# Expert rows of a two-layer mixture kernel: scattered by slot through HBM instead of gathered by one-hot matmuls, with a new order of the dense ranks and of the weight splitting

## What is computed

```python
def moe(h, p):
    t = h.reshape(B * L, D)
    scores = jax.nn.sigmoid(jnp.dot(t, p['router_w'], preferred_element_type=F32))
    biased = (scores + p['router_b'].astype(F32)).reshape(-1, N_GROUPS, epg)
    grp = jnp.argmax(lax.top_k(biased, TOP_K)[0].sum(-1), -1)
    in_grp = jnp.take_along_axis(biased, grp[:, None, None], axis=1)[:, 0]
    _, local = lax.top_k(in_grp, TOP_K)
    expert = grp[:, None] * epg + local
    w = jnp.take_along_axis(scores, expert, -1)
    w = ROUTE_SCALE * w / w.sum(-1, keepdims=True)
    combine = (jax.nn.one_hot(expert, N_EXPERTS, dtype=F32) * w[..., None]).sum(1)
    hid = jax.nn.silu(jnp.einsum('td,edf->tef', t, p['moe_w_gate'])) * jnp.einsum('td,edf->tef', t, p['moe_w_up'])
    y = jnp.einsum('tef,efd->td', hid * combine[..., None].astype(hid.dtype), p['moe_w_down'])
```

## Time and profile before

| | value |
|---|---|
| median of three runs | 1816.57 us |
| the profiled execution's own time | 1820.26 us |
| its span | 1818.1 us |
| mean granted TensorE clock | 0.911 of full speed |
| TensorE (PE) busy | 1561.1 us, 86% |
| VectorE (DVE) busy | 903.4 us, 50% |
| ScalarE (ACT) busy | 720.1 us, 40% |
| GpSimd (POOL) busy | 189.1 us, 10% |
| moved by DMA | 271.78 MB, mean 149 GB/s |

### The profile page before, as it was taken

The page is one execution under the profiler, slowest core; times in us unless marked ns, Lnnn a source line. Parts: engine busy times, 40 slices in busy tenths (PEclk is TensorE's granted clock), DMA queues, the critical chain, the costliest instruction groups (busy, mean ns, idle before and its releaser), DMA issues.

```text
span 1818.1 us, 29285 instructions
## 1 busy us (share of the span) xinstructions
PE 1561.1 (86%) x9368; PEld 1291.0 (71%) x9368; DVE 903.4 (50%) x1591; ACT 720.1 (40%) x1215; POOL 189.1 (10%) x226
## 2 busy tenths in 40 slices
PE   6999988889996698888779999898899958898884
PEld 4888877676885576666568789777678747676672
DVE  1754634424346544565837445443343474545656
ACT  3453334341244434455244433434222453435543
POOL 0010100000000532101000110000000013430010
PEclk9999988899998699999859989888999978999896
DMA  9412143432351247876262222435233404668640
GB/s 343 141 62 90 47 172 114 168 110 98 116 182 35 110 157 244 317 265 233 88 254 105 70 70 95 148 117 180 75 128 122 165 1 151 215 231 328 246 152 35
DMA packets 74523, 271.78 MB, mean 149 GB/s; under 512 B 9452, under 2 KB 9756, under 8 KB 72832
## 3 DMA queue, kind: packets, MB, share of 16 engines
q1 hardware_dynamic: 66384, 236.79, 37.0%
q0 software_dynamic: 7984, 33.07, 4.8%
HBM read 254.97 MB, written 16.19 MB: 149 GB/s over the span
## 4 chain that ended last, share of the span: by engine, by line
PE 58%; DVE 17%; DMA 8%; ACT 6%; issue 4%; DVEq 4%; ACTq 1%; SPq 0%; POOL 0%; POOLq 0%
PE psum L982 6%; PE psum L983 6%; PE psum L984 6%; PE psum L1359 4%; DMA ring<-units_in 4%; PE psum L1539 3%; DVE ring_lo L2217 3%; PE psum L1480 3%; DMA ring<-units_ada 3%; PE psum L1481 3%; PE psum L1482 3%; DVE ring_lo L2308 2%; ACT w_hi L1765 2%; PE psum L1518 1%; PE psum L1001 1%
## 5 line engine op out<-in xcount | busy, mean ns | idle before, releaser
L2308 DVE TENSOR_TENSOR ring_lo<-ring,u_hi 128x1024 fp32r<-128x1024 f32 x116 | 143.8, 1239 | 329.2 <-ACTq L1849 325.0
L982 PE MATMUL psum<-x_hi,u_hi 128*128 128x384 f32 x736 | 264.1, 359 | 21.4 <-DVEq L2310 10.8
L984 PE MATMUL psum<-x_hi,ring_lo 128*128 128x384 f32 x736 | 254.5, 346 | 0.0
L983 PE MATMUL psum<-x_lo,u_hi 128*128 128x384 f32 x736 | 254.5, 346 | 0.0
L1848 ACT ACTIVATE u_hi<-ring 128x1024 fp32r<-128x1024 f32 x116 | 122.8, 1058 | 280.7 <-DMA ring<-units_in 202.5
L982 PEld LDWEIGHTS psum<-x_hi,u_hi 128*128 128x128 f32 x736 | 145.2, 197 | 36.9 <-issue 11.5
L983 PEld LDWEIGHTS psum<-x_lo,u_hi 128*128 128x128 f32 x736 | 145.2, 197 | 1.5 <-issue 0.3
L984 PEld LDWEIGHTS psum<-x_hi,ring_lo 128*128 128x128 f32 x736 | 144.4, 196 | 0.0
L2217 DVE TENSOR_TENSOR ring_lo<-ring,w_hi 128x1024 fp32r<-128x1024 f32 x96 | 118.2, 1231 | 40.9 <-ACTq L1766 32.8
L1765 ACT ACTIVATE w_hi<-ring 128x1024 fp32r<-128x1024 f32 x96 | 101.7, 1059 | 42.0 <-PE psum L1520 24.3
L1061 PE MATMUL psum<-ring,condS 128*32 128x128 f32 x1536 | 68.6, 320 | 39.3 <-DMA ring<-units_ada 37.8
(11 more groups left out here) (415 smaller groups left out, 3222.5 us busy)
## 6 DMA issues: line engine op xcount, KB each, us to landing
ring<-units_moe SPq DMA_DIRECT2D x132, 512.0 KB, 5.2
ring<-units_in SPq DMA_DIRECT2D x116, 512.0 KB, 3.4
ring<-units_ada SPq DMA_DIRECT2D x96, 512.0 KB, 4.9
R<-units_moe SPq DMA_DIRECT2D x60, 512.0 KB, 6.4
ring<-units_br SPq DMA_DIRECT2D x32, 320.0 KB, 2.9
ring<-units_out SPq DMA_DIRECT2D x16, 512.0 KB, 3.3
expert_out_rows<-RE POOLq DMA_DIRECT2D x12, 512.0 KB, 6.5
prm<-params SPq DMA_DIRECT2D x2, 1304.0 KB, 10.0
```

The costliest lines, as they stand in the source:

```text
L982: mm(o, hi[:, c], x_hi[:, k, :], start=k == 0, stop=False)
L983: mm(o, hi[:, c], x_lo[:, k, :], start=False, stop=False)
L984: i = mm(o, lo[:, c], x_hi[:, k, :], start=False, stop=k == DT - 1)
L2308: V.tensor_tensor(ring_lo[:, slot_of(u), :], ring[:, slot_of(u), :, :].rearrange("p a b -> p (a b)"), u_hi[:, n % 2, :].bitcast(F32), ALU. ...
```

## The change

The one-hot gather, its constants and matrices, and the stage `hl` are gone. In their place:

- The stage `hb` turns the unsplit rows (24 transposes) into `h2_rows`. VectorE writes the integer slots, and POOL scatters all rows by slot into an HBM tensor, `slot_rows`, with six indirect DMAs. It waits for all of them and then loads the rows of 15 tiles (12 of FULL ranks, 3 for all SMALL ranks) one after the other, three ahead, into `rows_in`. In the first layer the tensor is filled once with finite values, in 15 DMAs during the mixers, at the stage `rs`.
- Steps `("xt", x)` turn a tile by eight transposes on TensorE; ScalarE writes the high part and VectorE the low part (SMALL: one copy each for a half of the k-tiles).
- VectorE, not POOL, forms the low part of the dense rows (`low_of_h2`), in pieces between the routing steps.
- Rank 0 goes first, ahead of rank 2. Its down product times its weight becomes the accumulator `acc` (`take_first`). Rank 1 stays last.
- The step `back` stands behind the last rank's second gate-up half and ahead of its `tr`. VectorE alone adds the rows that came back, and the gated sum, for all three tiles.
- `rounded_at` skips steps whose units are all SMALL. So where the next rank is SMALL, the down units of a FULL rank are split at the rank's own `("gu", r, 1)`.
- Banks for the jobs are chosen by their count of jobs.

```diff
-ORDER = [2, 11, 3, 12, 4, 13, 10, 14, 5, 15, 9, 6, 8, 7, 0, 1]
+ORDER = [0, 2, 11, 3, 12, 4, 13, 10, 14, 5, 15, 9, 6, 8, 7, 1]
+FIRST, LAST = ORDER[0], ORDER[-1]
...
+def turned_in(before, r):
+    if r == FIRST:
+        return FULL_TILES[0:2]
+    if before == FIRST:
+        return SMALL_ROWS
+    q = ORDER[ORDER.index(r) + 1]
+    return [(q, t) for t in range(len(TILES[q]))] if q in FULL else []
...
 def expert_steps():
-    first, second = ORDER[:2]
-    s = [("ga", 1, 0, 4), ("ga", 1, 4, DT), ("gu", first, 0), ("gu", first, 1), ("ga", 0, 0, DT)]
-    for before, r in zip(ORDER[:-2], ORDER[1:-2]):
-        s += [("gu", r, 0), ("tr", before)] + ([("ga",) + FILL[r]] if r in FILL else [])
-        s += [("gu", r, 1), ("dn", before)]
-    before, r = ORDER[-3:-1]
-    s += [("gu", r, 0), ("tr", before), ("g2",), ("dn", before), ("gu", r, 1)]
-    s += [("gu", LAST, 0), ("back",), ("tr", r), ("dn", r), ("gu", LAST, 1)]
+    def turned(before, r):
+        return [("xt", x) for x in turned_in(before, r)]
+    s = [("gu", FIRST, 0)] + turned(None, FIRST) + [("gu", FIRST, 1)]
+    for before, r in zip(ORDER[:-2], ORDER[1:-1]):
+        s += [("gu", r, 0), ("tr", before)] + turned(before, r) + [("gu", r, 1), ("dn", before)]
+    before = ORDER[-2]
+    s += [("gu", LAST, 0), ("tr", before), ("dn", before), ("g2",), ("gu", LAST, 1), ("back",)]
     return s + [("tr", LAST), ("dn", LAST)]
...
 def rounded_at():
-    at = {i: [] for i in range(len(STEPS))}
-    with_units = [1] + [i for i, step in enumerate(STEPS) if step_units(step)]
+    at = {i: [] for i in range(-1, len(STEPS))}
+    with_units = [-1] + [i for i, step in enumerate(STEPS) if any(u in ROUND_AT for u in step_units(step))]
     for i, j in zip(with_units, with_units[1:]):
         at[i] = [u for u in step_units(STEPS[j]) if u in ROUND_AT]
...
+            def turn_tile(x):
+                i = ROW_AT[x]
+                pe.wait_ge(rows_loaded[i % IN_PLACES], nth(l, rows_loaded[i % IN_PLACES], 16 * (i // IN_PLACES + 1)))
+                for half, job in enumerate(step_jobs(("xt", x))):
+                    turn_rows(job, [rows_in[:, i % IN_PLACES, (4 * half + k) * P:(4 * half + k + 1) * P] for k in range(4)])
...
+                        if l == 0:
+                            for at in range(0, N_SLOT, P):
+                                n = min(P, N_SLOT - at)
+                                pool.dma_start(slot_rows[at:at + n, :], cst[0:n, 0:D]).then_inc(rows_cleared, 16)
...
-                for d in range(DT):
-                    pool.wait_ge(x_hi_ready, nth(l, x_hi_ready, DT + d + 1))
-                    nc.gpsimd.tensor_tensor(h_lo[:, d, :], h2[:, d, :], h_hi[:, d, :].bitcast(F32), ALU.subtract)
+                pool.wait_ge(back_ready, nth(l, back_ready, 2 * NT))
                 pool.wait_ge(slots_ready, nth(l, slots_ready, 1))
...
+                for t in range(NT):
+                    for x in range(2):
+                        n = x * NT + t
+                        pool.indirect_dma_start(
+                            out=slot_rows, out_offset=bass.IndirectOffsetOnAxis(ap=slot_i[:, n:n + 1], axis=0),
+                            in_=h2_rows[:, t, :], in_offset=None,
+                            bounds_check=N_SLOT - 1, oob_is_err=False).then_inc(scattered, 16)
+                pool.wait_ge(scattered, nth(l, scattered, 16 * 2 * NT))
+                for i in range(IN_PLACES):
+                    load_rows(i)
...
             def add_back(t):
-                dve.wait_ge(scaled_ready, nth(l, scaled_ready, t + 1))
                 dve.wait_ge(rows_back[t], nth(l, rows_back[t], 32))
+                dve.wait_ge(acc_ready, nth(l, acc_ready, t + 1))
+                for x in range(2):
+                    V.scalar_tensor_tensor(out=acc[:, t, :], in0=back_rows[x][:, t, :], scalar=wab[:, x, t:t + 1],
+                                           in1=acc[:, t, :], op0=ALU.mult, op1=ALU.add)
+                    dve.drain()
...
+            def gated_sum(t):
+                V.tensor_tensor(acc[:, t, :], acc[:, t, :], g2bc[:, min(t, 1), :], ALU.mult)
                 dve.drain()
-                V.scalar_tensor_tensor(out=X[:, t, :], in0=X[:, t, :], scalar=ALPHA, in1=acc,
+                V.scalar_tensor_tensor(out=X[:, t, :], in0=X[:, t, :], scalar=ALPHA, in1=acc[:, t, :],
                                        op0=ALU.mult, op1=ALU.add)
...
+            def take_turned(x):
...
+                for half, job in enumerate(jobs):
+                    dve.wait_ge(xg_hi_ready, nth(l, xg_hi_ready, 2 * i + half + 1))
+                    k = slice(4 * half, 4 * half + 4)
+                    V.tensor_tensor(lo[:, k, :].rearrange("p a b -> p (a b)"), psum[:, bank(job), :],
+                                    hi[:, k, :].rearrange("p a b -> p (a b)").bitcast(F32),
+                                    ALU.subtract).then_inc(drained[bank(job)], 1)
...
                 elif name == "rt":
+                    for d in range(3):
+                        low_of_h2(d)
...
+                    for d in range(3, 5):
+                        low_of_h2(d)
...
                     for x, v in enumerate((low, top)):
-                        V.tensor_tensor(hot_at[:, x, :, :], along(v).to_broadcast(pair),
-                                        across(route_const("chunk_base")).to_broadcast(pair), ALU.subtract)
+                        V.tensor_copy(slot_i[:, x * NT:(x + 1) * NT], v)
                     dve.drain().then_inc(slots_ready, 1)
...
+                    for d in range(5, DT):
+                        low_of_h2(d)
```

More of the change, by code:

```diff
@@ L181, in stages @@
           ("rl", [], ["rl"]),
[L182 to L184 removed]
+          ("hb", [], [f"hb{t}{h}" for t in range(NT) for h in range(2)]),
+          ("cn", [], ["cn"])]
     return s
@@ L263, in token_tiles @@
         return [(t * P, 0, P, None) for t in range(NT)]
-    c, off, width = CHUNK_OF[r], SLOT_OFF[r], HALF if r in SMALL else P
-    out, done = [], 0
-    while done < SPAN[r]:
-        at = min(off + done, CHUNK_W[c] - width)
-        if done:
-            at = min(at, max(off, off + SPAN[r] - width))
-        row = off + done - at
-        n = min(SPAN[r] - done, width - row)
-        out.append((at, row, n, CHUNK_BASE[c] + off + done))
-        done += n
-    return out
+    if r in SMALL:
+        at = min(SLOT_OFF[r], N_SMALL - HALF)
+        return [(at, SLOT_OFF[r] - at, CAP[r], SLOT_OFF[r])]
+    return [(0, 0, min(P, CAP[r] - at), SLOT_OFF[r] + at) for at in range(0, CAP[r], P)]
 TILES = {r: token_tiles(r) for r in range(N_EXPERTS)}
@@ L322 @@
 ROUNDED_AT = rounded_at()
-def gather_parts(c):
-    return ("x",) if CHUNKS[c] == SMALL else ("h", "l")
 def step_jobs(step):
@@ L333, in step_jobs @@
         return [f"tr{step[1]}.{t}" for t in range(len(TILES[step[1]]))]
-    if step[0] == "ga":
-        return [f"ga{step[1]}.{k}{x}" for k in range(step[2], step[3]) for x in gather_parts(step[1])]
+    if step[0] == "xt":
+        return [f"xt{ROW_AT[step[1]]}.{half}" for half in range(2)]
     if step[0] == "back":
@@ L483, in route_constants @@
     e = np.arange(N_EXPERTS)
[L484 to L486 removed]
+    base = [ABSENT * 2 if r in DENSE else SLOT_OFF[r] for r in range(N_EXPERTS)]
+    c = {"before": i < j, "ones": np.ones(P), "expert": e, "key_tie": N_EXPERTS - 1 - e,
+         "rank": e, "slot_base": np.array(base)}
     return np.ascontiguousarray(np.concatenate(
@@ L1455, in gate_up @@
                 jobs = step_jobs(("gu", r, 0))
-                c = CHUNK_OF.get(r)
-                if c is not None and part == 0:
-                    pe.wait_ge(xg_act, nth(l, xg_act, gathered(c, DT - 1)))
-                    pe.wait_ge(xg_dve, nth(l, xg_dve, gathered(c, DT - 1)))
+                if r == FIRST and part == 0:
+                    pe.wait_ge(x_hi_ready, nth(l, x_hi_ready, 2 * DT))
+                    pe.wait_ge(h_split, nth(l, h_split, DT))
+                elif r == SMALL[0] and part == 0:
+                    pe.wait_ge(xs_low_ready, nth(l, xs_low_ready, len(SMALL_ROWS)))
+                    pe.wait_ge(xs_high_ready, nth(l, xs_high_ready, len(SMALL_ROWS)))
+                elif r in FULL and part == 0:
+                    pe.wait_ge(xg_lo_ready, nth(l, xg_lo_ready, 2 * FULL_AT[r, len(TILES[r]) - 1] + 2))
                 for j in (2 * part, 2 * part + 1):
```

337 lines of the change are left out of this document (147 added, 190 removed).

## The result

The kernel after takes 1799.88 us, the median of nine executions (1793.09 to 1810.20 but for one of 6744 us), the kernel before 1815.97 in nine (1806.84 to 1819.86). The ratio is 0.9928 with a 95% interval of 0.9907 to 0.9949: 0.7% faster, some 13 us (the two medians lie 16 us apart). The forecast was 1785, 1.7% less than before. The sign and the range held; by the ratio less than half of the gain came.

The account below looks back on a forecast made before the run. Prediction: TensorE carries 58% of the chain of waits. Layer two -73.0 + 70.3 - 14.9 = -17.6, layer one -13.1, together -30.7 from 1820.26 gives 1789.6; that execution lay 3.7 above the median, so 1785, range 1750 to 1811.

Parts of the forecast that it names:

- The start: Routing to first gate-up: without a gather and with faster routing, rank 0's gate-up starts 12.7 us earlier.
- The tail: From rank 7's down product to rank 1's: 14.9 us less, though TensorE idles some 15 us of it.
- Rank 0 and the transposes: Added in the loop: rank 0's halves and down product 25.3 us, transposes of 15 row tiles 16.7 us.
- Ranks 9, 6, 8, 7: Late loop: these ranks get bound by VectorE, some 45 us against TensorE's 40; 6 us added with imperfect overlap.
- The new wait: Turns of ranks 3, 4, 10, 5: down units split ahead of silu land late; 8.8 us plus 3 of slow matmuls.
- DMA bound: Rival: bytes per pair of a one-tile and a small rank take 22.3 us against 20; total 1797, chance 0.08.
- landings at 8.8: Rival: loads land after 8.8 us in all eight stalls, 28 us more; total 1813, no change, chance 0.06.
- the wait for the first rows: Loop start: TensorE waits for scattered rows to be loaded back, 6 us plus 2 of slow matmuls.
- rows late: Rival: VectorE's splits block POOL's DMA starts, 5 us more per layer; total 1795, chance 0.14.
- the five waits: Removed in the loop: TensorE's waits for down units split beside SMALL ranks, 12.2 us plus 4.8 of slow matmuls.
- the small weight operations: Added in the loop: some 15 small VectorE operations now stand ahead of the copies of nine jobs, 2.5 us.
- The rival of the clock: Stalls leave TensorE's clock low for half a rank each, 28 us more per layer; total 1842, chance 0.09.

Follow-up runs that it names:

- c_order: Kernel after plus three follow-up edits (0.9689), with pairs holding one-tile ranks placed between pairs holding two-tile ranks: 1762.30 us, ratio 0.9702 to the kernel before.
- c_more_dma: Kernel after plus three follow-up edits (0.9689), with POOL storing 512 KB more at five down products: 1759.12 us, ratio 0.9681 to the kernel before.
- a_hold: Kernel after, but SyncE issues weight units 6 and on only once the rows are scattered: 1797.43 us, ratio 0.9900 to the kernel before.
- experiment 5: Kernel after, with weight units 6 and on held until the scatter has landed, the same run as a_hold: 1797.43 us, ratio 0.9900.
- experiment 2: Kernel before with only the new splitting rule, which skips steps whose units are all SMALL: 1817.69 us, ratio 1.0008 to the kernel before.
- experiment 1: Kernel after with the old splitting rule, FULL ranks' down units split beside the SMALL rank again: 1811.62 us, ratio 0.9992 to the kernel before.

## Why the prediction was right or wrong

**Right.** The start: gate-up of rank 0 begins 22.8 us after the routing product, that of rank 2 began 35.7 after it, 12.9 earlier (12.7 forecast). The tail: 15.6 less (14.9), with 16.8 us of idle TensorE ahead of the last product and VectorE full, as said. Rank 0 and the transposes: 11.1 for the cold half (8.4 and 2), 8.4 for its product, and 0.96 to 1.04 per row tile. Ranks 9, 6, 8, 7: waits of 9.5 and 3.2 of slow matmuls make 12.7. The same ranks had some 13.5 before, of which the forecast had taken off 5.6 as removed (2.4 of waits, 3.2 of slow matmuls): 4.8 more than its sum had left there, where it had added 6. The new wait has the form that I gave it: it stands at the turn of ranks 3, 4, 10 and 5, ScalarE waits for a unit's load ahead of silu, and no wait is left at their down products.

**Wrong: the size of the new wait.** This is the step that failed first: the form was right, the term was too small. It said that the second unit "lands 5.3 us later (3.1 to 8.8)" and took the median of the whole loop for it (its example even works out with 5.1). The waits were 2.9, 1.8, 7.0 and 4.5 at ranks 3, 4, 10 and 5, instead of 1.6 for each two-tile and 2.8 for each one-tile rank: 16.2 for 8.8, and with the slow matmuls behind them (4.3 for 3) 8 to 9 us more than the sum had. In layer one they were 2.9, 1.3, 6.1 and 4.8. The second down unit's landing explains most of it: 5.1, 4.2, 8.5 and 6.1 us after its issue. At rank 10, the worst, it was the last of five units that SyncE had issued within 4.3 us, and the DMA engines were full (412 GB/s, against the 327 that I took from the earlier trace rows as an average). The rest is a way from the landing to `hidden` that is 0.3 to 0.6 longer than summed, and TensorE, which comes to the turn 0.2 to 0.3 sooner. The median of a ring was the wrong price for a unit that is issued last in a burst. That the burst, and not some other backlog, makes rank 10's unit late was not tried by itself; c_order, which moved these ranks apart, did not make it land sooner. My rival "DMA bound" had 1797 and comes nearest to the time, but its mechanism, bytes over all the ranks, is not what c_more_dma shows. The rival "landings at 8.8" had the mechanism of rank 10, and met it at one rank of four.

**Wrong: the wait for the first rows.** Forecast 6 and 2 of slow matmuls, measured 10.2 and 2.5. Six issues took 9.5 instead of 8.1, and POOL's wait for the last landing 11.3 instead of 5.8. I had read 5.8 from indirect loads with no weight unit issued among them; here nine weight units, 4.7 MB, were issued from 1490.93 on and shared the engines. a_hold, with three of them held back, gives 6.0. The load of the rows was overpriced (4.0 for 6.5), which hid 2.5 of the error. The rival "rows late" had the right effect for the wrong reason: slow issues were only 1.4 of it. They exist, though: 1.97 us for the issue that lay beside low parts of VectorE, 1.00 for one that lay beside almost none. The Trainium skill (SBUF — State Buffer, Who interferes with whom) says that `tensor_tensor` was not seen to stall a DMA's start, and marks the reason as inferred; these rows and the earlier trace rows speak against it. The kind of instruction does not decide alone: the first issue lay beside subtractions of 384 columns, also with both inputs in SBUF, and took 1.05. Another page of the Trainium skill (DMA: Bandwidth & Descriptors, Queues, rings and completion order) says, of DMAs that SyncE and ScalarE issue, that the completion is written only after every earlier write of that DMA engine, across its queues. By the order of issue the trace does not show this for the scatters: the one issued at 1496.27 landed after 11.0 us, at 1507.2, the unit issued before it, at 1495.94, only after 13.1, at 1509.0. The bytes beside the scatters (experiment 5) explain the lateness without it.

**Not a further error, but a gain credited for the wrong reason: the five waits.** They were counted at 12.2 and 4.8, which is what they cost before, and that much did go: none is left at these places. Against the new wait of 11.8 this made the new rule look like a gain of some 5 us per layer by itself. In the old kernel it gives nothing (experiment 2), which is again the new wait priced too low. In the new one it gives 12 us (experiment 1), since behind the new row copies the old waits would have grown to 19.7. I had neither. A rule that moves a wait has to be priced in the kernel in which it will stand.

Together, layer two's loop came out 7.0 longer than in the first profile of before, where my sum had it 2.7 shorter. Of these 9.7 us the new wait has 8.7 and the rows 4.7; the other terms were 3.7 too high, 1.2 of it at ranks 9 to 7, and 1.6 in the small weight operations (2.5 in the sum; TensorE waited 0.9 behind them). Against the second profile of before the loop is 4.6 further off.

**Not forecast: the mixers.** 7.6 us came from a stretch that the change does not touch. The experts themselves, from the routing to the end of the last down product, gave 8 to 11 of the forecast 31 (2.4 or 3.4 in layer one, 9.0 or 4.5 in layer two, by the first or the second profile of before). The forecast compared with one execution, and that execution's layer two was the slow one.

The rival of the clock did not come: 0.891 over the span against 0.911 and 0.917, and the kernel was still faster.

## What to carry to other kernels

Price a transfer that gates a stall by the landings of the transfers issued just before that stall, not by the median of the stream, and ask what else has been issued in the ten microseconds before it: at rank 10 the landing was 8.5 us where the stream's median was 5.3, and the last scatter's 11.3 shrank to 6.0 with less beside it. When a wait moves to another place in in-order queues, compare the two orders as wholes, since everything behind the late unit inherits the wait (`silu_gate`, then `low_of_hidden`, then `take_out`); put the small operation that frees the other engine ahead of the one that waits for memory. An idle stretch of TensorE ahead of a busy VectorE is worth only what VectorE's chain gives: 17 us of it in each layer gave 8 to 11 in all.

## What was not expected of the hardware

- The last of six indirect stores of 128 rows was waited for 11.3 us after its issue with 4.7 MB of weight loads beside them, and 6.0 with three units held back; the stretch beside them moved 417 GB/s (1500 to 1510 us), the highest slice between 1620 and 1640 had 442.
- 512 KB of stores more per rank lengthened one wait by 0.4 to 1.1 us and the total by nothing that an interval of 10 us either way can show.
- The granted clock over 30 us of the same work was 0.73 in three profiles of kernels with the gather and 0.84 in three of kernels without it.
- Two executions of the kernel before differ by 5.1 us ahead of the first routing and by 4.5 in layer two's experts: a sum of 10 us can be checked against one profile only stretch by stretch, and better against two.
